# A transformer block on one core: the first loads reordered around the modulation weights

## What is computed

```
mod = silu(c) @ mod_w + mod_b            # mod_w: 1024 x 6144, six vectors of 1024
h   = rms_norm(x, norm1_g) * (1 + scale1) + shift1      # the first two of the six
z   = h @ w_in + b_in                    # w_in: 1024 x 6680
... three kinds of attention on slices of z, merged with gates, @ w_out
... a router and 32 experts (exp_w1: 1024 x 2048, exp_w2: 1024 x 1024 each)
... a second block (retention / LSTM-like mixers, two feed-forward nets)
```

## Time and profile before

| | us |
|---|---|
| median of 3 runs | 2087.66 (2085.15 to 2088.86) |
| the profiled execution: its own time | 2086.4 |
| its span | 2084.6 |
| PE busy | 1868.3 (90%) |
| DVE, ACT, POOL busy | 831.6, 479.1, 460.4 |
| HBM read | 590.10 MB, 284 GB/s over the span |

### The profile page before, as it was taken

The page is one execution under the profiler, slowest core; times in us unless marked ns, Lnnn a source line. Parts: engine busy times, 40 slices in busy tenths (PEclk is TensorE's granted clock), DMA queues, the critical chain, the costliest instruction groups (busy, mean ns, idle before and its releaser), DMA issues.

```text
span 2084.6 us, 30633 instructions
## 1 busy us (share of the span) xinstructions
PE 1868.3 (90%) x11378; PEld 1119.9 (54%) x11379; DVE 831.6 (40%) x1574; ACT 479.1 (23%) x945; POOL 460.4 (22%) x260
## 2 busy tenths in 40 slices
PE   6999999987999789777877899989999999989997
PEld 3767867421323222212222222387599988758996
DVE  2236543440211111011111111458467766736776
ACT  1222330210000000000000000222445543224443
POOL 0002200034324324432343234142000004500000
PEclk8999999998999889978889899999999999999999
DMA  9343686799989999999999999953276635524662
GB/s 354 120 162 140 253 256 229 300 425 426 426 364 402 426 426 424 426 427 425 425 425 427 424 401 406 410 176 112 48 218 185 185 121 156 178 81 121 181 181 91
DMA packets 189446, 592.12 MB, mean 284 GB/s; under 512 B 10595, under 2 KB 110754, under 8 KB 153412
## 3 DMA queue, kind: packets, MB, share of 16 engines
q1 hardware_dynamic: 187356, 588.74, 74.2%
q10 hardware_dynamic: 2024, 2.46, 0.4%
HBM read 590.10 MB, written 2.63 MB: 284 GB/s over the span
## 4 chain that ended last, share of the span: by engine, by line
PE 65%; DMA 17%; POOL 6%; DVE 6%; issue 3%; ACT 2%; SPq 1%; ACTq 0%; POOLq 0%; DVEq 0%
DMA upper<-in_exp_w 12%; PE psum L2425 12%; PE psum L2161 9%; PE psum L2438 5%; POOL upper L1164 5%; PE psum L1752 4%; PE psum L2205 4%; PE psum L1896 3%; PE psum L1762 3%; PE psum L1880 3%; PE psum L1925 3%; DMA ring<-in_exp_w 2%; PE psum L1845 2%; PE psum L2170 2%; DVE rounded_ring L2597 2%
## 5 line engine op out<-in xcount | busy, mean ns | idle before, releaser
L2943 DVE TENSOR_SCALAR upper<-psum 128x512 f32<-128x512 f32 (+1 forms) x34 | 23.0, 678 | 631.2 <-PE psum L2170 363.6
L2425 PEld LDWEIGHTS psum<-rounded_upper 128*128 128x128 f32 x2112 | 257.4, 188 | 3.6
L2425 PE MATMUL psum<-rounded_upper 128*128 128x256 f32 x2112 | 258.8, 282 | 0.0
L2170 PE MATMUL psum<-ring,tables 128*32 128x512 f32 x1152 | 167.4, 722 | 92.2 <-POOL ring L1158 63.4
L1158 POOL COPY ring<-upper 128x4096 f32<-128x4096 f32 x30 | 108.0, 3601 | 639.6 <-DMA upper<-in_exp_w 494.4
L1164 POOL COPY upper<-upper 128x2048 f32<-128x2048 f32 x120 | 222.7, 1896 | 48.2 <-PE psum L2205 40.3
L2161 PE MATMUL psum<-ring,tables 128*64 128x512 f32 x896 | 215.7, 638 | 19.1 <-POOL ring L1158 17.4
L1143 POOL CAST rounded_upper<-ring 128x1024 fp32r<-128x1024 f32 x66 | 83.2, 1269 | 467.0 <-PE psum L2425 174.8
L2161 PEld LDWEIGHTS psum<-ring,tables 128*64 128x64 f32 x896 | 66.1, 147 | 170.5 <-issue 141.6
L2170 PEld LDWEIGHTS psum<-ring,tables 128*32 128x32 f32 x1152 | 36.4, 126 | 219.6 <-issue 180.3
L1481 ACT ACTIVATE upper<-upper 128x512 f32<-128x512 f32 x32 | 20.2, 632 | 541.4 <-DVE upper L2943 541.4
(11 more groups left out here) (450 smaller groups left out, 2837.0 us busy)
## 6 DMA issues: line engine op xcount, KB each, us to landing
ring<-in_exp_w SPq DMA_DIRECT2D x97, 2048.0 KB, 20.5
upper<-in_exp_w SPq DMA_DIRECT2D x128, 1024.0 KB, 11.8
upper<-in_exp_w SPq DMA_DIRECT2D x31, 2048.0 KB, 17.6
ring<-in_ffn_w_up SPq DMA_DIRECT2D x88, 512.0 KB, 5.2
ring<-in_mod_w SPq DMA_DIRECT2D x12, 2048.0 KB, 11.4
ring<-in_w_in SPq DMA_DIRECT2D x12, 2048.0 KB, 9.4
ring<-in_ffn_w_down SPq DMA_DIRECT2D x44, 512.0 KB, 5.7
ring<-in_odd_w_in SPq DMA_DIRECT2D x8, 2048.0 KB, 11.9
```

What stands on the lines that cost most here:

```text
L2170: ins = pe.matmul(o[32 * r:32 * r + 32].rearrange("p (g n) -> p g n", g=2), rows[:, 0:FEW], gate_and_up(k, r), start=first, stop=last, til ...
L2425: ins = pe.matmul(bank[4 + b][:, T * g:T * g + T].rearrange("p (i n) -> p i n", i=NT), w[:, g, k, :], x[:, k], start=(k == m == 0), stop=( ...
```

## The change

Ten places, all in the start-up; nothing from job 1 on is different.

- SP issues `x` between panels 0 and 1 instead of after panel 1 and the small transfers.
- ACT's first transfer is only the first 256 columns of `const` (identity and ones, 0.13 MB); it then issues only the 3 small ones that the modulation needs (`c`, `norm1_g`, `norm2_g`). The other 24 and the rest of `const` (0.66 MB) are issued by SP behind panel 4, ahead of panel 5.
- The transposes of `rows` are split: the 24 rows of the three vectors at the start, all tables (`turn_rows`) after job 0. `cols` is filled in two parts, and ACT waits for the second part (`cols_ready` 2) before it empties job 0.
- The fillers before the modulation products are six of 256 columns instead of six and three of 512; there are new ones behind the first quarter (8) and the third (4). The transposes of `xn` move from behind the fourth quarter to behind the second.
- ACT writes its chunks of `hT` first and issues the 14 transfers after that.

```diff
+        row_loads, N_FIRST_ROWS = [], 3
...
             for q, pl in enumerate(panels[:n_panels]):
-                if q == 2:
-                    for dest, src in row_loads[1::2]:
+                if q == 1:
+                    sp.dma_start(x_res, a["x"]...).then_inc(x_in, 16)
+                if q == 5:
+                    for dest, src in row_loads[N_FIRST_ROWS:]:
                         sp.dma_start(dest, src).then_inc(rows_in, 16)
-                    sp.dma_start(x_res, a["x"]...).then_inc(x_in, 16)
+                    sp.dma_start(const[:, T:NCA], a["const_a"][:, T:NCA]).then_inc(rows_in, 16)
...
-            act.dma_start(const, a["const_a"]).then_inc(tables_in, 16)
-            for dest, src in row_loads[0::2]:
-                act.dma_start(dest, src).then_inc(rows_in, 16)
+            act.dma_start(const[:, 0:T], a["const_a"][:, 0:T]).then_inc(tables_in, 16)
+            for dest, src in row_loads[0:N_FIRST_ROWS]:
+                act.dma_start(dest, src).then_inc(tables_in, 16)
...
-            act.wait_ge(mod0_done, 4)
+            act.wait_ge(mod_ready, 1)
+            for q in (0, 2):
+                act.wait_ge(x_turned, q + 1)
+                ...                                  # ACT's four chunks of hT
...
-            mod_bias(1, 3, x_in)
             act.dma_start(cmp_w2, ...).then_inc(cmp_in_sem, 16)
-            act.wait_ge(mod_ready, 1)
-            ...                                      # ACT's four chunks of hT
+            mod_bias(1, 3, x_in)
+            act.wait_ge(cols_ready, 2)
...
-            pe.wait_ge(tables_in, 16)
-            keep_busy(bank[1], 6)
-            pe.wait_ge(rows_in, 16 * len(row_loads))
-            ...                                      # four transposes of rows
+            pe.wait_ge(tables_in, 16 + 16 * N_FIRST_ROWS)
+            pe.transpose(bank[2][:, 0:ROW_B], rows[0:ROW_B, 0, :], ident[0:ROW_B, 0:ROW_B]).then_inc(rows_turned, 1)
+            def turn_rows():
+                pe.wait_ge(rows_in, 16 * (len(row_loads) - N_FIRST_ROWS + 1))
+                ...                                  # four transposes of rows
...
-            keep_busy(bank[1], 3)
+            keep_busy(bank[1], 6, T)
             pe.wait_ge(silu_ready, 1)
             for c in range(4):
                 mod_rows(bank[3], mod0[c], c).then_inc(mod0_done, 1)
-            pe.wait_ge(xn_ready, 1)
-            ...                                      # 16 transposes of xn
+                if c == 0:
+                    keep_busy(bank[1], 8, T)
+                if c == 1:
+                    pe.wait_ge(xn_ready, 1)
+                    ...                              # 16 transposes of xn
+                if c == 2:
+                    keep_busy(bank[1], 4, T)
...
             for n in range(first_a):
                 run_job(n)
+                if n == 0:
+                    turn_rows()
...
-            dve.wait_ge(tables_in, 16)
             dve.wait_ge(rows_turned, 1)
-            chained(dve.tensor_copy(cols, bank[2][:, 0:N_COLS]))
-            ...                                      # halving, cols_ready 1
+            dve.tensor_copy(cols[:, 0:ROW_B], bank[2][:, 0:ROW_B]).then_inc(cols_ready, 1)
...
+            dve.wait_ge(rows_turned, 2)
+            chained(dve.tensor_copy(cols[:, ROW_B:N_COLS], bank[2][:, ROW_B:N_COLS]))
+            ...                                      # halving, cols_ready 2
```

More of the change, by code:

```diff
@@ L908, in row @@
             row_loads.append((rows[at:at + n, table, sub], src))
-        row_loads = []
+        row_loads, N_FIRST_ROWS = [], 3
         row(ROW_C, 8, flat(a["c"][0], P))
@@ L1215, in _ @@
             act.activation(rstd, sumsq, ACT.Sqrt).then_inc(std_ready, 1)
-            act.wait_ge(mod0_done, 4)
+            act.wait_ge(mod_ready, 1)
+            for q in (0, 2):
+                act.wait_ge(x_turned, q + 1)
+                for k in (2 * q, 2 * q + 1):
+                    act.activation(hT[:, k, :], bank[4 + q][:, T * (k % 2):T * (k % 2) + T], ACT.Identity,
+                                   scale=scale1[:, k:k + 1], bias=mod[:, k:k + 1]).then_inc(hT_act, 1)
+            act.dma_start(start_const, a["const_s"]).then_inc(const_in, 16)
+            act.dma_start(lam_row, a["diff_lambda"].rearrange("o a b -> o (a b)").to_broadcast([P, 256])).then_inc(const_in, 16)
+            act.dma_start(sinks, a["sinks"].to_broadcast([P, 8])).then_inc(const_in, 16)
             at = 0
@@ L1684, in _, with keep_busy @@
         def _(pe):
-            def keep_busy(o, products):
+            def keep_busy(o, products, n=512):
                 for _ in range(products):
-                    pe.matmul(o, ones, const[:, 0:512], start=True, stop=True)
-            pe.wait_ge(tables_in, 16)
-            keep_busy(bank[1], 6)
-            pe.wait_ge(rows_in, 16 * len(row_loads))
-            at = 0
-            for n, (table, count_) in enumerate(((0, N_ROWS), (1, N_FROWS), (2, N_FROWS), (3, N_ROWS_O + 64))):
-                ins = pe.transpose(bank[2][:, at:at + count_], rows[0:count_, table, :], ident[0:count_, 0:count_])
-                at += count_
-            ins.then_inc(rows_turned, 1)
+                    pe.matmul(o[:, 0:n], ones, const[:, 0:n], start=True, stop=True)
+            pe.wait_ge(tables_in, 16 + 16 * N_FIRST_ROWS)
+            pe.transpose(bank[2][:, 0:ROW_B], rows[0:ROW_B, 0, :], ident[0:ROW_B, 0:ROW_B]).then_inc(rows_turned, 1)
+            def turn_rows():
+                pe.wait_ge(rows_in, 16 * (len(row_loads) - N_FIRST_ROWS + 1))
+                at = 0
+                for n, (table, count_) in enumerate(((0, N_ROWS), (1, N_FROWS), (2, N_FROWS), (3, N_ROWS_O + 64))):
+                    ins = pe.transpose(bank[2][:, at:at + count_], rows[0:count_, table, :], ident[0:count_, 0:count_])
+                    at += count_
+                ins.then_inc(rows_turned, 1)
             def mod_rows(target, q, c, alone=False):
```

28 lines of the change are left out of this document (10 added, 18 removed).

## The result

| | before | after |
|---|---|---|
| median, us | 2089.07 (2085.15 to 2098.27, 20 runs) | 2094.49 (2088.87 to 2100.25, 20 runs) |
| profiled execution, its own time | 2086.4 | 2095.71 |
| its span | 2084.6 | 2093.9 |

The ratio is 1.0025 (95% interval 1.0016 to 1.0035): the change made the kernel slower by a quarter of a percent, 5 us, where 8.7 us less were forecast (2079.0 against 2087.66). The median of before, now over 20 runs, lies 1.4 above that of the three in the prediction.

A forecast was written before the change was run, and what follows sets the result against it. It took PE's chain, behind a start-up bound by panel loads and ACT's issuing, as the bound. Terms -4.6 - 0.8 - 2.9 + 0.9 - 2.8 + 1.25 + 0.96 = -8.0 led to 2078.4 or 2079.7, forecast 2079.0 us; range 2075 to 2085.

The forecast's parts named there:

- nothing in the kernel is tied to absolute time: Expert loop: loads are released by engines, so they move with the start and its -8.0 us reaches the end.
- whatever moves the first job should move the mixer by as much: From 40 to 300 us: PE bounds the chain without DMA, so a gain at job 0 carries on in full.
- Rival 4: Expert loop: a full DMA queue takes the earlier start back, ending at about 2087 us; chance 0.08.
- the sum of the start: Start-up up to job 4's first weight load, 56.97 us before: all terms together make it 8.0 us earlier.
- the wait for rows: Between job 0 and the transposes of rows: PE waits 1.25 us for rows_in.
- The last modulation panel: Start-up loads: with fewer bytes ahead it lands at 27.5 us, 4.6 earlier; bounds 26.1 and 29.
- Panel 4: Job 0's weights: landing 5.4 us behind panel 3, at 32.9, they make job 0 wait 0.9 us, until 33.0.
- rival 1: Job 0 or 1 meets the 0.50 clock: -5.2 us, 2081.2; -3.6 with last quarter and turn slow too; chance 0.15.
- The main case: Whole start: job 0 at 33.0 us and full clock, 3.45 us for job 0, -8.0 in all; chance 0.66.
- turn_rows: After job 0: 24 small transfers (3.1 us) and 0.66 MB (1.7) complete rows_in at 37.7; transposes cost 0.96 us.
- the limit of 42: Start-up: the forecast calls itself wrong if rows_in comes after 42 us.
- rival 3: Start-up: 24 small transfers at 0.85 us each make PE wait 18.5 us, +9.3, ending at 2095.7; chance 0.05.

The follow-up runs named there:

- e1: Kernel before with 38 idle TensorE instructions added ahead of its start-up wait for the small transfers; 2101.5 us, ratio 1.0048.
- e6: Kernel before with the same 38 instructions as e1, put in front of the router at about 387 us; 2103.29 us, ratio 1.0063.
- e2: Changed kernel with nine start fillers fewer, leaving 2 instructions more than the kernel before; 2087.83 us, ratio 0.9989.
- e5: Changed kernel with 218 small PE instructions more at its start, 256 beyond the kernel before; 2087.93 us, ratio 0.9997.
- e4: Changed kernel with nine fillers fewer and the rest nearer to job 0 (0, 2 and 7 instead of 6, 8 and 4); 2084.82 us, ratio 0.9991.
- e8: e9 with the 24 small transfers issued by ACT instead of SP; 2087.72 us, ratio 0.9999.
- e9: e4 with turn_rows waiting only for the 24 rows, and DVE waiting later for the rest of const; 2084.03 us, ratio 0.9978.
- e11: The same program as e9, run once more unchanged; 2085.54 us, ratio 0.9975.
- e10: e9 with 31 tiny products and a transpose more, 128 instructions beyond the kernel before; 2087.49 us, ratio 0.9997.
- e3: Kernel before with only ACT's chunks of hT moved ahead of its 14 transfers; 2087.25 us, ratio 0.9984.
- e7: Kernel before with 32 tiny products (128 instructions) more in the start-up's idle time; 2091.3 us, ratio 1.0009.
- e12: Kernel before with 10 tiny products (40 instructions) more in the start's idle time; 2097.04 us, ratio 1.0034.

## Why the prediction was wrong

**The step that failed** is a sentence of the first part: "nothing in the kernel is tied to absolute time", and with it "whatever moves the first job should move the mixer by as much", carried on to the end. Something is tied, though not to time: the place of TensorE's code in its blocks is tied to the number of instructions ahead of it. The prediction costed the fillers at nothing, because the waits for panels cover them. That is right where they run, and wrong 540 us later: 38 instructions cost 7.3 us there. e1 and e6 show it without the change, e2 and e5 take it away from the change. The medians say 10 us for e1 and 13 for e6; their profiled executions lie 4 and 7 us under those medians, so the profiles don't show the rest. None of the rivals was this one. Rival 4 had the gain not carried, but for a full DMA queue and with an end at 2087, not behind the kernel before.

That step gives the sign. With the start's 4.0 and the branch's +7.3 the account gives +3.3; measured were +5, and the 2 us between are not settled. It isn't the only step: with the stall as before (e2) the changed kernel is at 2087.8, and that is outside the range too. **The second step that failed is the sum of the start**, -8.0 forecast and -4.0 measured. Its terms, forecast and in the changed kernel: job 0 begins at 33.0 and did at 35.6 (+2.6), takes 3.45 and took 6.39 (+2.9), the wait for rows 1.25 and none seen (-1.25), the transposes 0.96 and 0.51 (-0.45), the three jobs behind 10.35 and 10.4.

**The last modulation panel**: 29.6 against 27.5, beyond the upper bound of 29. The bytes were right. In the stretches, 0.94 + 3.67 + 2.1 and 9.6 us at 407 GB/s make 10.6 MB by 29.6; forecast were 9.84 and 0.65. The rate was wrong: 367 GB/s in 5 to 15 us and 407 from 20 us on, 394 on average, not 422 throughout. The slow stretch is the one in which `x` is now in flight together with `mod_b` from ACT's queue; that this is the reason was not tried. Panel 4 landed 5.9 us behind panel 3, at 35.5, where 5.4 and 32.9 were forecast, and that is when job 0 could begin.

**The clock**: rival 1 happened, and at its dear end; that its -3.6 is near the measured -4.0 is in part luck, since it has panel 3 on time and a wait for rows that wasn't there. The last quarter took 2.49 against 1.97 in before, the turn 1.13 against 0.6, job 0 6.39 against 3.45 forecast. The main case had "no gap should reach the 4 us that came before 0.50"; the clock fell in spite of smaller ones. From rows it can only be said what went before: the changed kernel and e2 had PE busy 7.8 and 6.9 of the ten us in 20 to 30, and a clock of 0.55 in the next ten; e4, e5, e8, e9 and e11 had it busy for all ten, and 0.83, 1.00, 1.00, 1.00 and 0.83. e10 breaks the pattern, with 8.0 and 1.00. The prediction took the new fillers for cover. Seven of them behind the third quarter (e4, e9) kept PE busy all through 20 to 30; but e5 has the changed kernel's fillers in their old places, with 54 tiny products ahead of them, and a clock of 1.00 too. So where fillers must stand is not shown.

**turn_rows**: the wait was not visible, but only because job 0 was slow and ended at 42.0. `rows_in` was complete at 41.1 (e4), against 37.7, inside the limit of 42 that I had set and 3.4 late. The transfers were priced as bytes in a queue that issuing never holds up. In the trace SP was in its first 11 small issues until 28.0 and needed 5 us for the other 13, so that `const` was issued only at 33.2; and it was then 8.2 us in flight (e4), where 1.7 were in the sum.

**Right in mechanism**: job 0 waits for w_in once ACT's issues are out of the way (e3, e9); ACT's 14 transfers behind hT cost nothing; turning xn earlier takes it off the path; small transfers are not the slow rival 3. e9's -7.6, with the clock held and `const` not waited for, is near the -8.0 in part by luck: its job 0 began 1.8 us later than forecast, and the wait and the transposes that had been counted were shorter by as much.

**Carrying**: of e9's 7.6 us, 4.6 and 5.2 arrive at the end, by the two ratios. In its profile 2 to 3 us go in 145 to 190 us, where the lower clock takes a longer share than in the profile of before (0.77 in 155 to 165 against 0.83, 0.71 in 180 to 190 against 1.00). But the one profile of before is an early one. The five profiles with the old start and ACT's old order reach the first product of the pass at 571.57 (before), 575.89, 577.29, 576.74 and 577.05 (e1, e6, e7, e12), 575.7 in the mean; after, e2 and e5 at 571.8, and e4 and e8 to e11 at 569.6 in the mean. By these the start's gain is largely carried to the pass: of 5.2 and 6.3 us that these two groups are ahead when the jobs end, 3.9 and 6.1 are left there. What takes the changed kernel's gain away comes with the pass. e3 doesn't fit: 5.4 us earlier at the jobs, and at the pass at 575.34. From the pass's first product to the end of the span the four profiles with a stall of about 4 us or more (after, e1, e6, e12) take 1517.5 to 1523.3 us, 1520.1 in the mean, the other ten 1511.2 to 1519.9, 1514.0 in the mean. So about 6 us of the branch's loss reach the end. With scatter of several us from profile to profile these means are rough; why e5 and e8 end without a gain stays open.

## What to carry to other kernels

When an edit adds or removes instructions ahead of a branch that is taken late and for the first time, look at that branch in the new profile. In this case it was code being fetched where the engine's own waits (not only the chain) named "issue" for more than 1 us and a `q8 instruction` packet was in flight in the same stretch. Pad both kernels to the same count before you compare them; here 38 to 40 idle instructions cost 7 to 13 us. A count that takes the stall from one branch can put it at another (e10). And fillers are not free because they run in idle time.

A single profile of a program of this length can be 14 us from the next one of the same program; read in it where something happens, and take the size from many runs.

## What the hardware showed that was not expected

- The stall at the first use of the branch: 1.0 to 4.8 us by layout, none with 128 instructions more. The next block's packet starts 2.4 to 3.0 us behind the first product of the pass and takes only about 1.1 us of one DMA engine (1.7% of 16 engines over 4.0 us); PE goes on 1.3 to 1.5 us behind it.
- Stalls of 1.0 to 1.7 us left the granted clock at 1.00, stalls of 4.0 to 4.8 us were followed by 0.54 to 0.81 in 580 to 590 us, and the second effect was the larger one: 4.9 of 7.3 us.
- One of this kernel's float32 fillers, a single line of code, counts as two products and two weight loads in the page, so that 32 of the tiny ones are 128 instructions; a transpose counts as one of each.
